# A hand-ordered fp32 transformer stack on one core: waits placed behind ready work, the decay product on row halves, and a new order at the start

## The chip, the cores and the metric

The kernel runs on one core of one Trainium2 chip, in fp32 throughout. The metric is the time of one execution on the device in microseconds (us). TensorE is called PE here, its weight loads PEld, VectorE DVE, ScalarE ACT, GpSimd POOL, SyncE SP. Each engine runs its own instruction list in order; semaphores tie the lists together.

## The reference, cut to what matters

256 tokens of width 1024 go through three layers. The first has an attention with a bias by distance, a pooling branch and a convolutional feed-forward part; the second ("even") has a forgetting attention ("fox", 8 heads) and a sliding-window attention with sinks ("swa", 8 heads), then a feed-forward part; the third ("odd") has an attention over the keys that an index score selects, then a mixture of 8 experts. Each layer's norm is modulated by vectors computed from a conditioning row `c` (the "ada" weights).

```python
def even_layer(x, c, cos, sin, ada_w, ada_b, ...):
    sh_m, sc_m, g_m, sh_f, sc_f, g_f = ada_modulation(c, ada_w, ada_b)
    h = rms_norm_2(x, norm_mix) * (1 + sc_m) + sh_m
    fq, fk, fv, fgl, sq, sk, sv = _split(h @ w_in, EVEN_SPLITS)
    log_f = jax.nn.log_sigmoid((fgl + forget_b).astype(jnp.float32))
    o_fox = forgetting_attention(heads(fq), heads(fk), heads(fv), log_f)   # scores + cumulated log_f
    o_swa = sliding_window_sink_attention(apply_rope(heads(sq), cos, sin), apply_rope(heads(sk), cos, sin), heads(sv), sinks)
    x = x + g_m * (jnp.concatenate([o_fox, o_swa], axis=-1) @ w_out)
    h = rms_norm_2(x, norm_ffn) * (1 + sc_f) + sh_f
    return x + g_f * swiglu(h, ffn_gate, ffn_up, ffn_down)
# odd_layer: q, k, v, iq, ik, iw = split(h @ w_in); o = dsa_attention(...);
#            x + g_f * moe_swiglu(h, ...), the sum over 8 experts of gate * swiglu
```

## The kernel before

Activations stand transposed: 8 chunks of 128 features by 256 tokens (`x`, `h`). Weights come through a ring of 24 slots of 512 KB, which SP fills in a fixed order and PE frees. A "unit" is a projection onto 128 features: 8 matmul blocks of 128x256, one per chunk of `h`. An fp32 matmul is two passes, and the trace counts each pass as one matmul. Results go to PSUM banks; ACT mostly copies them out (`take`, L1367) and so frees the bank.

The order of the work is written by hand, one program for each engine; units and the banks they use are numbered in `plan_units`. The places that matter here, with the lines of the profile:

- **Start.** SP first loads the conditioning row, the table of columns `cols` and the positions, then `x`, the identity, and the ring. DVE computes the angles of the rotation in a chain of ten operations that each wait for the one before (L1985 to L1993), then the sums of squares (L1712), then for each chunk c two modulation columns (L1728; each waits for one ring slot) and the product of `x` with the norm (L1717). ACT takes sine and cosine (L1524 to L1528), loads the table of Sqrt (L1373), takes the norm's root (L1400), and then scales and shifts each chunk into `h` (L1416). PE sums the squares (L767), multiplies the bias table (L1014), spreads the norm over the partitions (L777), and begins the q and k projections (L1024) as the chunks of `h` come. The chunks are not used evenly: with the first four chunks come 4, 12, 8 and 8 passes, and after chunk 3, 16 passes that need no later chunk.
- **Attention** (`attend`). Per pair of heads: scores (L865), for fox a second product that adds the decay (L872, 72 partitions deep, of which rows 0 to 7 and 64 to 71 carry data), softmax on DVE and ACT, transposes of the probabilities (L881), values (L894, L898). Other units (`between`) and the first steps of the output projection (`early_out`, L826) are put between. In the last turns there are no more scores to compute, and both transposes of neighbouring heads stand with nothing between them.
- **Raw units** (`raw_units`): after a feed-forward part the first two units of the next layer are multiplied with the unnormed input (L786) while the norm's sum (L767) and spread (L777) are made. The 8-wide products "fgl" and "iw" (L732, with a transpose, L747) come right after.
- **Odd attention.** Eight units "dq" are rotated: ACT makes four shifted copies of the bank (L1633), then takes the bank (L1367), and DVE rotates (L1825 to L1829); DVE also picks the keys (L2131, L2134).
- **Experts** (`expert_pass`): 8 passes; at the end of pass 0 DVE copies the turned selection (L2367) and then turns the hidden rows (L2244), which the next pass's first product on PE (L1283) waits for.

## Time and profile before

| quantity | value |
|---|---|
| median of 3 runs | 1267.29 us (1265.4 to 1267.48) |
| the profiled execution | 1263.85 us |
| its span in the trace | 1262.2 us |
| PE busy | 1229.3 us (97%) |
| DVE, ACT, POOL busy | 671.6 us (53%), 277.8 us (22%), 88.5 us (7%) |
| bytes moved by DMA | 368.78 MB, mean 292 GB/s |

The profiled execution is one execution; it took 3.4 us less than the median of the three runs. Its span is 1.65 us shorter than its time. In rows of the timeline the columns are start, duration, engine, line, operation, output<-inputs, size, count of merged instructions, and in brackets the idle time just before and what ended it. The ends of matmuls are modelled: eight passes given as 0.93 us are followed by the next row 0.86 us after their start.

### The profile page before, as it was taken

The page shows a single profiled execution, that of the slowest core. Times are in us where ns is not written, and L with a number is a line of the kernel's source. Part 1 is how long each engine was busy: PE and PEld are TensorE (multiplying, and loading weights), DVE is VectorE, ACT ScalarE, POOL GpSimd, SP SyncE. Part 2 cuts the span into 40 slices and gives each one's busy share as a digit, 9 for nine tenths or more (in the row PEclk, how much of TensorE's full clock was granted, in tenths as well). Part 3 has the DMA queues.
Part 4 walks back from the last instruction along what each step waited for, and adds up shares of the span by engine and source line. Part 5 has one row for each costly group of instructions (what it writes and reads, how often), then busy time and mean ns, then how long its engine had stood idle before and what let it go on. Part 6 is the DMA issues. An engine that isn't in the chain of part 4 may idle for free.

```text
span 1262.2 us, 26659 instructions
## 1 busy us (share of the span) xinstructions
PE 1229.3 (97%) x10620; PEld 936.9 (74%) x10620; DVE 671.6 (53%) x1672; ACT 277.8 (22%) x739; POOL 88.5 (7%) x157
## 2 busy tenths in 40 slices
PE   6999999999999999999999999999999999999997
PEld 4758888999999767789999997776654455455445
DVE  5455563888888735546776777883541011101104
ACT  4332203212111414540000004275300000000001
POOL 0100000000000000000000000100021100110120
PEclk9999999999999999999999999999999999999999
DMA  9999884577777583146777785795599999999993
GB/s 355 414 399 412 334 283 149 176 273 269 267 276 277 199 314 103 34 167 217 260 277 278 269 316 186 296 375 128 222 383 396 420 399 397 400 422 399 397 399 151
DMA packets 74822, 368.78 MB, mean 292 GB/s; under 512 B 8740, under 2 KB 8996, under 8 KB 49979
## 3 DMA queue, kind: packets, MB, share of 16 engines
q1 hardware_dynamic: 56594, 271.22, 57.3%
q0 software_dynamic: 18160, 96.64, 20.2%
q8 instruction: 45, 0.74, 0.2%
q14 instruction: 23, 0.18, 0.0%
HBM read 347.76 MB, written 20.06 MB: 291 GB/s over the span
## 4 chain that ended last, share of the span: by engine, by line
PE 92%; DVE 3%; DMA 2%; ACT 1%; SPq 1%; issue 1%; DVEq 0%
PE banks L957 21%; PE banks L697 16%; PE banks L1283 13%; PE banks L944 12%; PE banks L1332 9%; PE banks L1307 5%; PE banks L722 4%; PE banks L826 2%; PE banks L786 2%; PE banks L1024 2%; PE banks L881 1%; DMA side<-ada 1%; PE banks L865 1%; DMA ring<-stream 1%; PE banks L894 1%; DVE side L1728 1%
## 5 line engine op out<-in xcount | busy, mean ns | idle before, releaser
L1728 DVE CUSTOM_DVE_ANT_0 side<-side 128x1024 f32<-128x1024 f32 x128 | 151.1, 1220 | 32.6 <-DMA side<-ada 32.5
L1283 PE MATMUL banks<-ring,arena 128*32 128x512 f32 x1536 | 166.3, 592 | 1.6 <-DVE arena L2244 1.6
L944 PE MATMUL banks<-arena,ring 128*128 128x256 f32 x704 | 158.6, 379 | 0.0
L944 PEld LDWEIGHTS banks<-arena,ring 128*128 128x128 f32 x704 | 130.7, 190 | 16.1
L697 PE MATMUL banks<-h,ring 128*128 128x256 f32 x640 | 141.8, 380 | 0.3
L1283 PEld LDWEIGHTS banks<-ring,arena 128*32 128x32 f32 x1536 | 51.5, 110 | 111.4 <-issue 110.2
L697 PEld LDWEIGHTS banks<-h,ring 128*128 128x128 f32 x640 | 120.4, 190 | 18.4 <-issue 2.2
L2347 DVE TENSOR_TENSOR arena<-arena,banks 128x256 f32<-128x256 f32 (+1 forms) x48 | 15.2, 330 | 179.0 <-ACT arena L1665 178.9
L697 PE MATMUL banks<-arena,ring 128*128 128x256 f32 x384 | 84.3, 380 | 0.7 <-ACT arena L1464 0.5
L957 PEld LDWEIGHTS banks<-h,ring 128*128 128x128 f32 x672 | 81.4, 192 | 2.2
L614 POOL DMA_DIRECT2D side<-ada x64 | 34.0, 532 | 687.7 <-DVE msum L1728 678.2
L957 PE MATMUL banks<-arena 128*128 128x128 f32 x672 | 81.9, 275 | 0.0
L957 PE MATMUL banks<-arena,ring 128*128 128x128 f32 x672 | 81.9, 275 | 0.0
L957 PE MATMUL banks<-h,ring 128*128 128x128 f32 x672 | 81.8, 275 | 0.0
L697 PEld LDWEIGHTS banks<-arena,ring 128*128 128x128 f32 x384 | 72.5, 190 | 11.8 <-DVE x L1838 1.0
L1665 ACT ACTIVATE arena<-banks 128x256 f32<-128x256 f32 (+1 forms) x48 | 13.5, 318 | 303.4 <-PE banks L1283 253.1
L957 PEld LDWEIGHTS banks<-arena 128*128 128x128 f32 x672 | 78.4, 192 | 0.0
L957 PEld LDWEIGHTS banks<-arena,ring 128*128 128x128 f32 x672 | 78.4, 192 | 0.0
L1503 ACT ACTIVATE arena<-banks 128x128 f32<-128x128 f32 x42 | 11.7, 278 | 263.6 <-PE banks L957 263.6
L1307 PE MATMUL banks<-ring,arena 128*32 128x192 f32 x1536 | 63.9, 326 | 0.0
L1332 PE MATMUL banks<-side,arena 128*32 128x256 f32 x1152 | 63.7, 379 | 0.0
L1307 PEld LDWEIGHTS banks<-ring,arena 128*32 128x32 f32 x1536 | 51.6, 110 | 15.1 <-issue 4.7
(332 smaller groups left out, 1553.3 us busy)
## 6 DMA issues: line engine op xcount, KB each, us to landing
ring<-stream SPq DMA_DIRECT2D x247, 512.0 KB, 5.5
ring<-experts SPq DMA_DIRECT2D x96, 1024.0 KB, 18.9
side<-ada POOLq DMA_DIRECT2D x64, 1024.0 KB, 7.6
side<-experts SPq DMA_DIRECT2D x24, 1024.0 KB, 20.5
arena<-experts SPq DMA_DIRECT2D x8, 1024.0 KB, 21.9
yrows<-side POOLq DMA_DIRECT2D x1, 6144.0 KB, 42.7
hrows<-side POOLq DMA_DIRECT2D x1, 5632.0 KB, 23.4
arena<-lasts SPq DMA_DIRECT2D x8, 512.0 KB, 22.2
```

The costliest lines, as they stand in the source:

```text
L614: pool.dma_start(ada_slot[:, v % 2, :], ada[bass.ds(v + 8 * i, 1)].rearrange("a p r n -> p (a r n)")).then_inc(ada_full[v % 2], 16)
L697: last = pe.matmul(bank(u, a, a + T), ring[:, s, (k0 + kc) * P:(k0 + kc + 1) * P], moving[:, kc, :], start=(kc == 0), stop=(kc == kn - 1))
L722: last = pe.matmul(bank(u, at, at + width), h[:, kc, tile * P:(tile + 1) * P], ring[:, s, (kc % per) * width:(kc % per + 1) * width], star ...
L786: ins = pe.matmul(banks[:, b, 0:RAW], ring[:, pos % RING, k * P:(k + 1) * P], raw[:, k, :], start=(k == 0), stop=(k == KC - 1))
L826: last = pe.matmul(bank(u, (c % 2) * T, (c % 2 + 1) * T), ring[:, u.pos % RING, k * P:(k + 1) * P], moving[:, k, :], start=(k == 0 and c % ...
L944: last = pe.matmul(banks[:, 4 + c // 2, (c % 2) * T:(c % 2 + 1) * T], ring[:, s, c * P:(c + 1) * P], hid[:, j % 2, :], start=first and c % ...
L957: last = pe.matmul(banks[:, b, at * P:(at + 1) * P], weights[:, k * P:(k + 1) * P], moving[:, k, :], start=(start and k == 0), stop=(stop ...
L1024: ins = pe.matmul(bank(u, (n % 2) * T, (n % 2 + 1) * T), ring[:, u.pos % RING, k * P:(k + 1) * P], h[:, k, :], start=(k == 0 and n % 2 == ...
L1283: ins = pe.matmul(banks[BLOCK * j:BLOCK * (j + 1), t, :], hg[:, t, k, :], ring[:, m, (j % 2) * 512:(j % 2 + 1) * 512], start=(k == 0), sto ...
L1307: ins = pe.matmul(banks[BLOCK * j:BLOCK * (j + 1), BLOCKS + t, 0:2 * NARROW], hg[:, t, k, :], flat[:, at:at + 2 * NARROW], start=(k == 0), ...
L1332: ins = pe.matmul(banks[BLOCK * q:BLOCK * (q + 1), 6 + t // 2, (t % 2) * T:(t % 2 + 1) * T], mhidT[:, t, BLOCK * c:BLOCK * (c + 1)], moe_s ...
L1728: dve.tensor_tensor_reduce(weights, weights, cond[:, 0 if layer0 else 1, :], 1.0, 0.0, ALU.mult, ALU.add, accum_out=msum[:, n:n + 1]).then ...
```

## The change

Eight edits, all in the order or the shape of instructions, none in what is computed:

1. Start: SP loads `x` and the identity ahead of `cols` and the positions. The angle chain on DVE goes from the head of its list to behind the columns and norm of chunk 2. PE spreads the norm ahead of the bias table product. ACT does the root and all of `scale_shift(0)` before sine and cosine.
2. First attention: transposes of a pair's first head stand ahead of the gate units while scores of a later pair remain; ACT's order follows.
3. Raw units: two more blocks of the second unit stand ahead of the wait for the norm's squares; one whole unit goes ahead of "fgl" ("iw"), and another ahead of its transpose.
4. Fox decay: 40 rows for each head instead of 72, a pair's two heads in different halves of the partitions (rows 0 to 39 and 64 to 103), and one matmul of each head in turn. The data are laid out as for L865, whose two heads also stand in different halves.
5. The wait for the taken values `fv` goes from ahead of the even attention to the first fox pair's values.
6. Last turns of the even and odd attention: a step of `early_out` stands between the two transposes; the last step is split in two halves of its columns around the values.
7. `take_query`: ACT first takes the bank, and makes the four shifted copies from the copy in SBUF.
8. First expert pass: DVE turns the hidden rows before it copies the selection.

```diff
@@ start: SP, PE, ACT, DVE
             sp.dma_start(condrow, cond_d[0:1, :]).then_inc(cond_in, 16)
-            sp.dma_start(cols[:, :], cols_d).then_inc(cols_in, 16)
-            sp.dma_start(posi, pos_d).then_inc(cols_in, 16)
             sp.dma_start(x[:, 0:4, :], xT[:, 0:4, :]).then_inc(x_in, 16)
...
             sp.dma_start(mats[:, 0:P], mats_d[:, 0:P]).then_inc(ident_in, 16)
+            sp.dma_start(cols[:, :], cols_d).then_inc(cols_in, 16)
+            sp.dma_start(posi, pos_d).then_inc(cols_in, 16)
...
+            pe.wait_ge(ident_in, 16)
+            norm_spread(0)
             pe.wait_ge(s_bias, 16)
             pe.matmul(banks[:, 7, :], table[:, 512:], table[:, 0:512], start=True, stop=True).then_inc(s_early, 1)
-            pe.wait_ge(ident_in, 16)
-            norm_spread(0)
...
-            act.wait_ge(s_rope_dve, 9)
+            act.wait_ge(consts_set, 2)
+            load_table(ACT.Sqrt)
+            root(0)
+            act.wait_ge(s_rope_dve, 1)
+            scale_shift(0)
+            act.wait_ge(s_rope_dve, 10)
             act.activation(sin[:, :], ang, ACT.Sin).then_inc(s_rope_act, 1)
...
                 norm_chunks(0, c, c + 1)
+                if c == 2:
+                    angles()
@@ raw units
+                for k in range(2):
+                    raw_block(b.bank, b.pos, r, k)
                 begin(U["stat", r])
                 norm_sum(r)
...
             raw_units(2, ("fq", 0), ("fq", 1))
+            one(("fq", 2), r=2)
             few_outputs("fgl", 2)
-            one(("fq", 2))
+            one(("fq", 3))
             few_per_token("fgl")
-            one(("fq", 3))
             feature_units("fk", 4)
@@ fox decay
                     for a in pair:
-                        for lo, hi, n in ((0, HALF, HALF), (HALF, TRI, T)):
-                            ins = pe.matmul(banks[:, score_bank(a.n), lo:hi], cum[:, n - HALF:n], sel[:, a.i, 0:n],
-                                            start=False, stop=bool(lo))
+                        rows = slice(64 * a.half, 64 * a.half + 40)
+                        ins = pe.matmul(banks[:, score_bank(a.n), 0:HALF], cum[rows, 0:HALF], sel[rows, a.chunk, 0:HALF],
+                                        start=False, stop=False)
+                    for a in pair:
+                        rows = slice(64 * a.half, 64 * a.half + 40)
+                        ins = pe.matmul(banks[:, score_bank(a.n), HALF:TRI], cum[rows, HALF:T], sel[rows, a.chunk, 0:T],
+                                        start=False, stop=True)
                         ins.then_inc(s_score, 1)
@@ attend: transposes and steps
-                    first = heads is first_heads
-                    if 1 <= m <= len(pairs) and not first:
+                    steps = between.get(2 * m, []) + between.get(2 * m + 1, [])
+                    ahead = m + 1 >= len(pairs)
+                    if 1 <= m <= len(pairs) and not ahead:
                         transposes(pairs[m - 1][0])
-                    for step in between.get(2 * m, []) + between.get(2 * m + 1, []):
+                    for step in steps[:1] if m > len(pairs) else steps:
                         step()
-                    if 1 <= m <= len(pairs) and first:
+                    if 1 <= m <= len(pairs) and ahead:
                         transposes(pairs[m - 1][0])
                     if m >= 2:
                         values(pairs[m - 2])
+                    for step in steps[1:] if m > len(pairs) else []:
+                        step()
@@ take_query on ACT
-                act.wait_ge(*u.done)
+                take(u, dqT[:, c, :], 0, T)
+                act.wait_ge(*taken(u))
...
-                    act.activation(ropet[to, c % 3, :], banks[at, u.bank, 0:T], ACT.Copy, scale=1.0 if j % 2 else -1.0).then_inc(s_shift, 1)
-                take(u, dqT[:, c, :], 0, T)
+                    act.activation(ropet[to, c % 3, :], dqT[at, c, :], ACT.Copy, scale=1.0 if j % 2 else -1.0).then_inc(s_shift, 1)
@@ first expert pass on DVE
+                rows_turned(p)
                 if first:
                     dve.wait_ge(s_picktr, 2)
                     dve.tensor_copy(pickT[:, :, P:T], banks[:, 4, 0:BLOCKS * P].rearrange("p (a n) -> p a n", n=P)).then_inc(s_pickT_dve, 1)
-                rows_turned(p)
```

DVE's list, the start of the kernel before: the angle chain (`arena`, `half_pi`, `negsink`) stands first, then `ghalf`, the sums of squares and the first modulation column.

```order
L1985 CAST arena<-arena 128x256
L1986 TENSOR_SCALAR arena<-arena,vectors 128x256
L1987 TENSOR_SCALAR arena<-arena 128x256
L1988 TENSOR_SCALAR arena<-arena 128x256
L1990 SCALAR_TENSOR_TENSOR arena<-arena 128x256 x3
L1991 TENSOR_SCALAR arena<-arena 128x256
L1992 MEMSET half_pi 128x1
L1993 TENSOR_SCALAR negsink<-vectors 128x8
L1995 SCALAR_TENSOR_TENSOR ghalf<-vectors 128x8
L1712 TENSOR_TENSOR h<-h 128x256 x6
L1728 ISA ring,msum<-ring,side 128x1024
```

DVE's list of the changed kernel around the same chain, from the norm product of chunk 2 (L1733 there) to the first column of chunk 3 (L1744 there).

```order
L1733 TENSOR_TENSOR h<-x,banks 128x256
L2001 CAST arena<-arena 128x256
L2002 TENSOR_SCALAR arena<-arena,vectors 128x256
L2003 TENSOR_SCALAR arena<-arena 128x256
L2004 TENSOR_SCALAR arena<-arena 128x256
L2006 SCALAR_TENSOR_TENSOR arena<-arena 128x256 x3
L2007 TENSOR_SCALAR arena<-arena 128x256
L2008 MEMSET half_pi 128x1
L2009 TENSOR_SCALAR negsink<-vectors 128x8
L1744 ISA ring,msum<-ring,side 128x1024
L1744 ISA msum 128x1
```

The whole chain now stands between chunk 2's norm product and chunk 3's two columns.

ACT's list of the kernel before, where the copies of q and k end (L1541, L1542), the first half of v is taken (L1367) and the root of the q and k norms follows (L1549).

```order
L1541 ACTIVATE arena<-banks 128x256
L1542 ACTIVATE arena<-banks 128x256
L1367 ACTIVATE arena<-banks 128x512
L1549 ACTIVATE var<-banks,eps 128x512 x2
L1367 ACTIVATE arena<-banks 128x512
```

The same place on ACT in the changed kernel (L1557, L1558, L1382 and L1565 there).

```order
L1557 ACTIVATE arena<-banks 128x256
L1558 ACTIVATE arena<-banks 128x256
L1382 ACTIVATE arena<-banks 128x512
L1565 ACT_TABLE_LOAD
L1565 ACTIVATE var<-banks,eps 128x512 x2
L1382 ACTIVATE arena<-banks 128x512
```

Since sine and cosine now come after the Sqrt of the norm, the compiled list holds a second load of the Sqrt table at this place (and one of the sine's table ahead of the sine).

PE's list of the kernel before, from the norm's squares in the even layer's raw units (L767) to the units fq 3 and fk 0 to 3 (the last row merges them).

```order
L786 MATMUL banks<-logit,ring 128x257 x6
L767 MATMUL banks<-ones,h 128x1 x4
L786 MATMUL banks<-logit,ring 128x257 x4
L777 MATMUL banks<-constants,var 128x128 x2
L786 MATMUL banks<-logit,ring 128x257 x6
L732 MATMUL banks<-h,vectors 32x256 x8
L697 MATMUL banks<-h,ring 128x256 x8
L747 MATMUL banks<-constants,logit 128x8 x2
L697 MATMUL banks<-h,ring 128x256 x40
```

The same place on PE in the changed kernel (every line here is one higher: L787, L768, L778, L733, L698, L748).

```order
L787 MATMUL banks<-logit,ring 128x257 x8
L768 MATMUL banks<-ones,h 128x1 x4
L787 MATMUL banks<-logit,ring 128x257 x4
L778 MATMUL banks<-constants,var 128x128 x2
L787 MATMUL banks<-logit,ring 128x257 x4
L698 MATMUL banks<-h,ring 128x256 x8
L733 MATMUL banks<-h,vectors 32x256 x8
L698 MATMUL banks<-h,ring 128x256 x8
L748 MATMUL banks<-constants,logit 128x8 x2
L698 MATMUL banks<-h,ring 128x256 x32
```

One full unit (8 blocks) moved ahead of the 8-wide product and one ahead of its transpose, and two raw blocks moved ahead of the norm's sum.

## Rows read from the trace of the kernel before

**Rows 1.** The page, part 4: the chain that ended last, by engine.

```profile
PE 92%; DVE 3%; DMA 2%; ACT 1%; SPq 1%; issue 1%; DVEq 0%
```

**Rows 2.** Timeline, DVE, the start: angle chain and modulation columns.

```profile
4.80 0.29 DVE L1985 CAST arena<-arena 128x256 f32<-128x256 int32 x1 [4.80 <-DMA arena<-positions]
...
8.00 0.17 DVE L1993 TENSOR_SCALAR negsink<-vectors 128x8 f32<-128x8 f32 x1
...
24.43 1.22 DVE L1728 CUSTOM_DVE_ANT_0 ring<-ring,side 128x1024 f32<-128x1024 f32 x1
...
26.72 0.42 DVE L1717 TENSOR_TENSOR h<-x,banks 128x256 f32<-128x256 f32 x1
...
29.35 1.23 DVE L1728 CUSTOM_DVE_ANT_0 ring<-ring,side 128x1024 f32<-128x1024 f32 x1 [2.21 <-DMA ring<-stream]
```

**Rows 3.** Timeline, PE, the q and k projections.

```profile
18.86 5.85 PE L1024 MATMUL banks<-h,ring 128*128 128x256 f32 x16 [1.30 <-ACT h L1416]
25.29 1.99 PE L1024 MATMUL banks<-h,ring 128*128 128x256 f32 x8 [0.58 <-ACT h L1416]
27.91 22.71 PE L1024 MATMUL banks<-h,ring 128*128 128x256 f32 x104 [0.63 <-ACT h L1416]
```

**Rows 4.** Windows at the end: busy time by engine, then PEclk, DMA share, GB/s.

```profile
1254.90:1258.80 3.90, 0.00 (x0) 0.00 (x0) 3.59 (x8) 3.07 (x12) 0.00 (x0) 1.00 0.16 61
1258.90:1262.20 3.30, 0.00 (x0) 0.00 (x0) 0.78 (x2) 0.00 (x0) 0.00 (x0) 0.50 0.63 234
```

**Rows 5.** Timeline: the q and k norms' first root, and a table load later.

```profile
58.40 0.69 ACT L1549 ACTIVATE var<-banks,eps 128x512 f32<-128x512 f32 x1 [0.27 <-PE banks L1045]
59.13 0.30 PEld L722 LDWEIGHTS banks<-ring,h 128*128 128x128 f32 x2 [0.23 <-ACT var L1549]
...
82.56 1.28 ACT L1564 ACT_TABLE_LOAD   x1
83.86 1.06 ACT L1564 ACTIVATE side<-side 128x1024 f32<-128x1024 f32 x1
```

**Rows 6.** Timeline, ACT and PE, after the first raw units; and the page, part 5.

```profile
433.00 4.04 ACT L1416 ACTIVATE h<-h,mod,avec 128x256 f32<-128x256 f32 x8 [2.54 <-DVE h L1717]
...
434.99 2.73 PE L732 MATMUL banks<-h,vectors 128*32 128x256 f32 x16
...
L1332 PE MATMUL banks<-side,arena 128*32 128x256 f32 x1152 | 63.7, 379 | 0.0
```

**Rows 7.** Timeline, PE, the first fox pair: scores and decay.

```profile
474.76 0.93 PE L865 MATMUL banks<-arena 64*128 64x128 f32 x8 [0.92 <-ACT arena L1367]
475.62 1.58 PE L872 MATMUL banks<-arena 72*128 72x128 f32 x8
```

**Rows 8.** Timeline, PE, the even attention's last turns.

```profile
525.43 0.52 PE L881 MATMUL banks<-constants,logit 128*128 128x128 f32 x3 [0.67 <-ACT logit L1443]
...
536.49 1.78 PE L826 MATMUL banks<-arena,ring 128*128 128x256 f32 x7 [0.51 <-ACT arena L1464]
```

**Rows 9.** Timeline, PE, the first attention.

```profile
118.92 0.52 PE L881 MATMUL banks<-constants,logit 128*128 128x128 f32 x3 [0.67 <-DVE logit L1781]
```

**Rows 10.** Timeline, DVE and PE, from the first rotated query to the first transposes.

```profile
818.37 0.43 DVE L1825 TENSOR_TENSOR arena<-arena,sin 128x256 f32<-128x256 f32 x1 [2.63 <-ACT arena L1633]
...
833.12 0.55 PE L881 MATMUL banks<-constants,logit 128*128 128x128 f32 x3
```

**Rows 11.** Timeline, ACT and PE, where the odd layer's output projection begins.

```profile
850.14 1.57 ACT L1633 ACTIVATE arena<-banks 32x256 f32<-32x256 f32 x4
...
852.22 1.10 PE L826 MATMUL banks<-arena,ring 128*128 128x256 f32 x4 [1.30 <-issue]
```

**Rows 12.** Timeline, expert pass 0 to 1; and the page, part 5.

```profile
950.39 0.56 DVE L2367 COPY arena<-banks 128x384 f32<-128x384 f32 x1 [14.34 <-PE banks L1317]
...
951.97 2.35 PE L1283 MATMUL banks<-ring,arena 128*32 128x512 f32 x20 [1.62 <-DVE arena L2244]
...
L1283 PE MATMUL banks<-ring,arena 128*32 128x512 f32 x1536 | 166.3, 592 | 1.6 <-DVE arena L2244 1.6
```

More of the change, by code:

```diff
@@ L818, in step @@
                     pe.wait_ge(s_o, pairs_done + k + 1)
-                    for c in range(4):
+                    for c in columns:
                         out_block(name, moving, c, k)
@@ L889, in values @@
                     pe.wait_ge(*taken(U["sv"]))
+                if pair[0].kind == "fox" and pair[0].i == 0:
+                    pe.wait_ge(*taken(U["fv", 0]))
+                    pe.wait_ge(*taken(U["fv", 1]))
                 if done >= 1:
@@ L1136, in _ @@
                        8: [sv_unit]}
-            for k in range(7):
+            for k in range(6):
                 m = max(5, 3 + k)
                 between[2 * m] = between.get(2 * m, []) + [early_out("eo", oT2, 4, k)]
+            between[18] = [early_out("eo", oT2, 4, 6, columns) for columns in ((0, 1), (2, 3))]
             attend(even_heads, between)
@@ L1194, in _ @@
             between = {2 * (c - 4): [dq(c)] for c in range(4, 8)}
-            for k in range(7):
+            for k in range(6):
                 m = max(4, 3 + k)
                 between[2 * m] = between.get(2 * m, []) + [early_out("oo", dqT, 12, k)]
+            between[18] = [early_out("oo", dqT, 12, 6, columns) for columns in ((0, 1), (2, 3))]
             attend(odd_heads, between)
@@ L1450, in attend @@
                         exps(pairs[m][0])
-                        if first:
-                            exps(pairs[m][1])
-                    if first:
+                    if first and m + 1 >= len(pairs):
                         for step in steps:
@@ L1457, in attend @@
                         transposed(pairs[m - 1][0])
-                    if m < len(pairs) and not first:
+                    if m < len(pairs):
                         exps(pairs[m][1])
+                    if first and m + 1 < len(pairs):
+                        for step in steps:
+                            step()
                     if m >= 2:
@@ L1608, in _ @@
             norm(4)
+            take(U["iq", 1], iqT[:, 1, :], 0, T)
             take(U["iw"], few, 0, T)
-            take(U["iq", 1], iqT[:, 1, :], 0, T)
+            take(U["iq", 2], iqT[:, 2, :], 0, T)
             take(U["iwT"], iws.rearrange("p a n -> p (a n)"), 0, 16, scale=float(8 ** -0.5 * 64 ** -0.5))
-            for c in range(2, 4):
-                take(U["iq", c], iqT[:, c, :], 0, T)
+            take(U["iq", 3], iqT[:, 3, :], 0, T)
             for c in range(2):
@@ L2449, in _constants @@
     pool = np.ascontiguousarray(pool.reshape(2, P, 4, T).transpose(1, 0, 2, 3))
-    sel = np.zeros((72, 8, T), np.float32)
-    sel[np.arange(8), np.arange(8)] = 1.0
-    sel[64 + np.arange(8), np.arange(8)] = 1.0
+    sel = np.zeros((FORGET, 4, T), np.float32)
+    for half in range(2):
+        for at in (64 * half, 64 * half + 32):
+            sel[at + half + 2 * np.arange(4), np.arange(4)] = 1.0
     inv_freq = (np.float32(10000.0) ** (-np.arange(32, dtype=np.float32) / np.float32(32))).astype(np.float32)
```

86 lines of the change are left out of this document (44 added, 42 removed).

## Prediction

> **What bounds the kernel now.** I read the chain that ended last first: TensorE's own work is 92% of it, and DMA, DVE and ACT together about 6% [rows 1]. So only two things can move the time: PE's own passes, and the places where PE stands idle for another engine. I then went along PE's timeline and took each idle stretch with what ended it. The stalls are many and small, 0.5 to 1.6 us each, and lie where the change works: before the first fox pair, between neighbouring transposes, at the start of the odd output projection, between expert passes 0 and 1 [rows 7 to 9, 11, 12]. The modelled ends of matmuls run a little late (0.93 us given for 0.86 us [rows 7]), so each idle shown is about 0.1 us too small. A full-rate 256-column pass is 22.71/104 = 0.218 us [rows 3]; a block is 0.44, a unit of 8 blocks 3.5 us.
>
> **The start: a loss, +3.4 us.** Before, the angle chain runs from 4.80 to 8.17, 3.4 us, while DVE has nothing else to do but wait for the load of x [rows 2]. After, it stands between the norm product of chunk 2 and the columns of chunk 3. Does a wait hide it there? In the rows of before DVE starts the column of chunk 3 at 24.43, with no idle ahead of it, and ends the norm product of that chunk at 27.14; ACT's scaling follows and PE starts on chunk 3 at 27.91 [rows 2, 3]. The ring had delivered already. The next wait for a slot, 2.21 us, comes only behind it, at 29.35 [rows 2]. So chunk 3 comes 3.4 us later, at 31.3. Chunk 4 is late by 3.4 less that wait, 1.2 us, and PE has 24 passes (5.2 us) of other work from chunk 3 to there, so only PE's start on chunk 3 counts. From there PE ran 104 passes without an idle [rows 3]: it cannot catch up, and all 3.4 us go into the end. The two first chunks come up to 2.7 us earlier (x first, no sine ahead of the norm's root), but chunk 2 waits for its ring slots in any case, so PE only idles elsewhere. Bounds: 0 (chain hidden) to +3.6 (ten linked operations with their gaps). I take 3.4.
>
> **A table load on the path, +1.0 us.** The compiled order of the changed kernel loads the Sqrt table between the take of v's first half and the root of the q and k norms. Before, ACT stands idle 0.27 us there, starts the root at 58.40, and PE's next weight load waits for it (0.23 us) [rows 5]. A load took 1.28 us [rows 5], less the idle of 0.27: +1.0. The other new load, ahead of the sine, comes when all chunks are scaled; what follows it on ACT is the copy of the bias rows, some 2.6 us late (the load and three activations of 256 columns), whose results are needed tens of us later. If that cover fails, it costs at most those 2.6 us.
> The Trainium skill ("ScalarE: Activation LUTs", section "What ACT_TABLE_LOAD costs") puts a drain of 1380 ns behind the load of 1283 ns, which speaks against the change: the term would be +2.4. The trace agrees on the load, but shows the next operation 0.02 us after the load's end [rows 5], so I leave the drain out.
>
> **First attention, -0.7.** A transpose of a second head waited 0.67 us for DVE with nothing between [rows 9]; the four gate units now stand between the two. Bounds 0 (a softmax late at the earlier place of the first head) and -0.8.
>
> **After the raw units, -2.6 in the even layer.** Eight chunks of h come from ACT between 433.00 and 437.04 [rows 6]. The 16 passes of the 8-wide product start at 434.99 and take 2.73 us [rows 6], though such a product, on 32 columns of the array, goes at 63.7/1152 = 0.055 us a pass when nothing holds it [rows 6], or 0.9 us: it is paced by ACT. Before, product and unit end at 434.99 + 2.73 + 3.5 = 441.2. After, the unit goes first, and its last block follows the last chunk: 437.04 + 0.44 = 437.5; then the product, 438.4. That is 2.8 us. The wait for the norm's squares, which the two raw blocks fill, lies inside this: the chunks come no earlier. Off goes up to 0.4 us where the next unit finds its bank just being copied. Taken -2.6, bounds -2.0 and -3.1.
>
> **The same place in the odd layer, -1.1.** The gain on PE is the same, but behind it DVE works through the key selection from 818.37 without a long break until the first transposes at 833.12 [rows 10]. That chain starts when ACT's shifted copies of the first query are there, and ACT now takes the bank first, 0.4 us more. Nothing kept is one bound, 2.6 - 0.4 = 2.2 the other; I see no row nearer to either, and take the middle.
>
> **Fox decay, -2.6.** The decay product took 1.58 us for a pair, and the scores of the same columns, with the two heads in different halves of the rows, 0.93 [rows 7]. Four pairs: 4 x 0.65 = 2.6. The trace shows no 40-row matmul; the bounds are nothing (two halves do not run side by side) and -2.6, and the nearest row is the score of the very same pair. DVE gets two small operations more for the sums and two for the table, of the size of work that it does in its idle half.
>
> **The wait for fv, -0.9.** The first pair waited 0.92 us for ACT's take [rows 7]. The values that need it come a whole pair later.
>
> **The ends of the attentions, -1.2 each.** In the even one: two stalls of 0.67 us between neighbouring transposes (at 525.43 and, alike, at 529.62) and 0.51 us ahead of the last output step [rows 8], 1.85 in all. A step of 4 blocks (1.8 us) now fills each. What is late next: the step itself waits for ACT's copy of the values just ahead, which was covered by a pair of transposes before; I put 0.3 us on each of two places. 1.85 - 0.6 = 1.2; bounds -0.4 and -1.9. The odd one shows the same pattern with the same idles. Together -2.4.
>
> **Start of the odd output projection, -1.3.** PE stands 1.30 us ahead of the first step [rows 11]. Its bank is that of the last query, and ACT's four shifted copies (1.57 us, to 851.7) come ahead of the take; with the take first, the bank is free about 1.5 us earlier. Bounds -0.8 and -1.5.
>
> **First expert pass, -1.6.** DVE stood 14.34 us idle, then copied the selection (0.56), then turned the rows, and PE waited 1.62 us for the turn [rows 12]. The turn needs only the gathered rows, and can lie in those 14 us; PE then needs only the selection's copy, and that later. If the rows land late, nothing is won. The weights are no obstacle: of 1536 matmuls that read them from the ring, all idle ahead is this 1.6 us [rows 12].
>
> **Sum.** +3.4 + 1.0 - 0.7 - 2.6 - 1.1 - 2.6 - 0.9 - 2.4 - 1.3 - 1.6 = -8.8. With about 0.1 us of hidden idle in each of nine stalls, -9.7. The profiled execution would go from 1263.85 to 1254.2; the median of the runs stands 3.4 us above the profiled execution, so 1267.29 - 9.7 = 1257.6. All bounds taken at their poor end (start +3.6, load and its cover +3.6, gains of 2.0, 0.8, 0.8 and 0.8 alone, after the raw units, at fv, at the two ends and at the output projection) give about +3; all at the good end about -16.
>
> **Rivals.**
> *The clock falls in the new gap.* PE idles from 27.3 (end of chunk 2 [rows 3]) to 31.3, 4.0 us. At the end of the kernel PE does nothing from 1254.9; the granted clock shows 1.00 to 1258.8 and 0.50 from 1258.9 [rows 4]: it fell to the lower of its two levels (1.2 of 2.4 GHz) 4.0 us after PE's last work. So the new gap is just at the edge. Price: the first 16 passes of the projections took 5.85 us [rows 3] where 3.5 is the full rate, 2.4 us for one climb. Time 1260.0. The Trainium skill ("TensorE: Matmul & The Clock Gate", section "HAM oscillation — how this bites in real kernels") warns against idle gaps of this order between bursts of matmuls, since the clock then falls; by that rule 1260.0 would be the forecast. The tail agrees that it falls, but shows a gap of the same length that did not yet do it.
> *The change does not cost at the start.* If chunk 3's slots come later than before (the ring's loads are issued behind two more small ones, or x first draws the bandwidth), the chain lies in that wait. Then 1254.2. Against it: chunk 3's columns found their slots there, and the same bytes are loaded ahead of them as before.
> *Stalls move instead of going.* The filled waits come back at the next step: each step or unit put in front ends in a bank that ACT must still copy, and the softmax of the next head is no earlier. If half of the 14.2 us of gains go so, the net is 4.4 - 7.1 = -2.7: 1264.6. For it speaks DVE's chain in the odd layer [rows 10].
> *Slower.* The clock falls in the gap and stays low. Each pass at the lower level costs 0.218 us more; all 104 passes up to the end of q and k would cost 22.7 us, 1280. It turns slower than before once 45 passes (9.7 us) run low, and by more than 0.2% from 56. Against it: the climb at 18.86 was over within 16 passes.
>
> **How the numbers follow.** The sum as it stands 0.50; clock falls once 0.20; no cost at the start 0.09; stalls move 0.15; slower 0.06. What a measurement of this kernel can tell from no change is 0.2%, 2.5 us. Faster: the first three cases and half of the fourth, 0.87; within 0.2%: the other half, 0.08; slower 0.05. The range 1251 to 1264 takes the first three cases with their bounds and the better part of the fourth.
>
> **What the profile after would show.** Right: PE's row of 104 passes starting near 31.3 with an idle of 4 us; an ACT_TABLE_LOAD just ahead of the q and k root, and PE's idle there near 1.2; the decay rows at about 0.9 a pair; no idle ahead of the first fox pair, the odd layer's first output step and pass 1 of the experts; PE's busy time less by 2.6 to 4. Wrong: passes of 0.43 us behind 31.3 (the clock); the columns of chunk 3 preceded by a wait for the ring (no cost); new idles ahead of L829's steps or of the unit behind each filled place (moved stalls). The forecast fails most easily at the fox term, if two 40-row halves don't run side by side, and at the four places where I trust ACT's copies to be early enough.

## The result and the profile after

The changed kernel takes 1256.93 us in the median of 4 runs (1255.1 to 1258.46), the kernel before 1266.89 beside it: a ratio of 0.9923, 95% interval [0.9905, 0.994], faster by 0.6 to 1.0%. A second set gave 1257.04 against 1266.53, ratio 0.992 [0.9904, 0.9936]; there one of twelve runs of the kernel before took 2159.77 us at a granted clock of 0.558 and is left out of its median. The forecast was 1257.6. The profiled execution took 1257.12, its span is 1255.5 us.

The page of the changed kernel, part 4, the chain by engine:

```profile
PE 90%; DVE 5%; DMA 3%; ACT 1%; issue 1%; SPq 1%; DVEq 0%; POOLq 0%; ACTq 0%
```

DVE has more of the chain than before [rows 1], and the timeline shows where. DVE and PE at the start, the counterpart of [rows 2, 3]:

```profile
20.28 1.23 DVE L1744 CUSTOM_DVE_ANT_0 ring<-ring,side 128x1024 f32<-128x1024 f32 x1 [2.27 <-DMA ring<-stream]
...
23.04 0.29 DVE L2001 CAST arena<-arena 128x256 f32<-128x256 int32 x1
...
26.44 1.22 DVE L1744 CUSTOM_DVE_ANT_0 ring<-ring,side 128x1024 f32<-128x1024 f32 x1
...
29.07 1.22 DVE L1744 CUSTOM_DVE_ANT_0 ring<-ring,side 128x1024 f32<-128x1024 f32 x1
```

```profile
23.90 1.99 PE L1037 MATMUL banks<-h,ring 128*128 128x256 f32 x8 [1.23 <-ACT h L1431]
29.93 25.16 PE L1037 MATMUL banks<-h,ring 128*128 128x256 f32 x104 [4.04 <-ACT h L1431]
```

The chain sits between 23.04 and 26.44, 3.4 us, and behind it the first column of chunk 3 starts with no wait; so does that of chunk 4, at 29.07. PE has an idle of 4.04 us ahead of chunk 3. The same 104 passes then take 25.16 us, not 22.71. The windows of that stretch (the last columns are PEclk, DMA share, GB/s) say why:

```profile
27.00:30.00 3.00, 0.07 (x1) 0.08 (x1) 3.00 (x6) 1.28 (x3) 0.00 (x0) 0.68 1.02 407
...
32.00:34.00 2.00, 2.00 (x6) 1.55 (x6) 0.58 (x1) 0.49 (x1) 0.00 (x0) 0.50 1.01 404
34.00:38.00 4.00, 4.00 (x18) 3.46 (x17) 3.95 (x8) 1.57 (x4) 0.00 (x0) 0.89 1.03 410
```

The granted clock fell to its lower level inside the idle and came back only after 34 us: PE did some 5 us of its passes at half rate.

The root of the q and k norms, answering [rows 5]; the load follows the take, and PE waits for the root 0.87 us:

```profile
62.61 1.28 ACT L1565 ACT_TABLE_LOAD   x1
...
63.90 0.69 ACT L1565 ACTIVATE var<-banks,eps 128x512 f32<-128x512 f32 x1
64.64 0.30 PEld L723 LDWEIGHTS banks<-ring,h 128*128 128x128 f32 x2 [1.27 <-ACT var L1565]
64.64 1.55 PE L723 MATMUL banks<-ring,h 128*128 128x512 f32 x3 [0.87 <-ACT var L1565]
```

The first attention, DVE and PE: the wait of [rows 9] is at another transpose, behind DVE columns that waited for an ada load.

```profile
122.52 1.23 DVE L1744 CUSTOM_DVE_ANT_0 side<-side 128x1024 f32<-128x1024 f32 x1 [4.86 <-DMA side<-ada]
...
125.62 0.55 PE L888 MATMUL banks<-constants,logit 128*128 128x128 f32 x3 [0.72 <-DVE logit L1797]
```

After the raw units of the even layer, ACT and PE, answering [rows 6]: the unit goes at full rate, the 8-wide product behind it takes 1.07 us, not 2.73, and no row of PE here waits.

```profile
438.35 4.04 ACT L1431 ACTIVATE h<-h,mod,avec 128x256 f32<-128x256 f32 x8 [2.54 <-DVE h L1733]
...
434.49 1.02 PE L768 MATMUL banks<-ones,h 128*128 128x1 f32 x8
...
439.38 3.77 PE L698 MATMUL banks<-h,ring 128*128 128x256 f32 x16
443.08 1.07 PE L733 MATMUL banks<-h,vectors 128*32 128x256 f32 x16
```

The first fox pair, answering [rows 7]: scores with no wait ahead, then the decay in two merged rows, and the next pair's scores 0.65 us after the decay's start, where it was 1.5.

```profile
476.76 0.93 PE L868 MATMUL banks<-arena 64*128 64x128 f32 x8
477.52 0.39 PE L875 MATMUL banks<-arena 40*128 40x128 f32 x4
477.74 0.60 PE L879 MATMUL banks<-arena 40*128 40x256 f32 x4
478.17 0.82 PE L868 MATMUL banks<-arena 64*128 64x128 f32 x8
```

The end of the even attention [rows 8]: the waits between transposes are gone, one is now ahead of an output step. In the odd layer the first transposes wait for DVE, and the first output step [rows 11] no longer waits.

```profile
527.90 1.99 PE L829 MATMUL banks<-arena,ring 128*128 128x256 f32 x8 [0.63 <-ACT arena L1480]
...
829.52 0.55 PE L888 MATMUL banks<-constants,logit 128*128 128x128 f32 x3 [0.50 <-DVE logit L1797]
...
847.15 3.19 PE L829 MATMUL banks<-arena,ring 128*128 128x256 f32 x14
```

Expert pass 0 and the step to pass 1 [rows 12], PE and DVE:

```profile
939.81 0.59 PE L1347 MATMUL banks<-side,arena 128*32 128x256 f32 x2 [0.73 <-issue]
...
945.31 3.21 PE L1298 MATMUL banks<-ring,arena 128*32 128x512 f32 x28
```

```profile
942.28 0.98 DVE L2269 STREAM_TRANSPOSE arena<-logit 128x768 f32<-128x768 f32 x1 [12.68 <-DMA logit<-hrows]
945.42 0.56 DVE L2393 COPY arena<-banks 128x384 f32<-128x384 f32 x1 [2.16 <-PE banks L1332]
```

DVE has the rows turned by 943.26, and PE starts pass 1 at 945.31. The gathered rows land only just before 942.3, so this edit had a margin of 2 us and not of 14.

**Where the time went.** The same instruction's start in both profiles, before and after, and what changed from one point to the next:

| place | before | after | difference | step |
|---|---|---|---|---|
| v's first pass (end of q and k) | 50.47 | 54.92 | +4.45 | +4.45 start |
| PE behind the q and k root | 59.15 | 64.64 | +5.49 | +1.04 table load |
| first unit after the first attention | 157.71 | 163.06 | +5.35 | -0.14 first attention |
| unit behind the transpose of fgl | 445.40 | 448.27 | +2.87 | -2.5 raw units, even |
| first fox scores | 474.76 | 476.76 | +2.00 | -0.9 wait for fv |
| transposes behind the fourth fox pair | 495.14 | 493.98 | -1.16 | -3.2 fox decay |
| last output step, even | 536.49 | 534.36 | -2.13 | -1.0 end of even attention |
| first transposes, odd | 833.12 | 829.52 | -3.60 | -1.5 raw units, odd |
| first output step, odd | 852.22 | 847.15 | -5.07 | -1.5 query taken first |
| last output step, odd | 877.60 | 871.27 | -6.33 | -1.3 end of odd attention |
| pass 1 of the experts | 951.97 | 945.31 | -6.66 | -0.3 (144 passes of pass 0 on weights in `side` held, +1.5; rows turned first -1.7; the rest of pass 0 -0.1) |

The held passes are those around the idle of 0.73 us: from their first row to the transposes behind them they take 9.36 us (930.98 to 940.34), and took 7.88 before (937.42 to 945.30).

The two profiled executions stand 6.7 us apart, the medians 10.0. The missing 3.3 us are looked for below.

### The profile page after: what moved, and what is told of

Its sections match the earlier page's. It is cut to its first block, busy times and chain, and to the rows that moved or that the text cites. A ratio compares the mean times of both kernels' runs of the same rounds, so it can differ in the third digit from the quotient of the medians.

```text
span 1255.5 us, 26666 instructions
## 1 busy us (share of the span) xinstructions
PE 1226.2 (98%) x10620; PEld 931.8 (74%) x10620; DVE 671.1 (53%) x1676; ACT 281.2 (22%) x741; POOL 88.4 (7%) x157
## 4 chain that ended last, share of the span: by engine, by line
PE 90%; DVE 5%; DMA 3%; ACT 1%; issue 1%; SPq 1%; DVEq 0%; POOLq 0%; ACTq 0%
PE banks L970 21%; PE banks L1298 13%; PE banks L698 13%; PE banks L957 12%; PE banks L1347 9%; PE banks L1322 5%; PE banks L723 4%; PE banks L829 2%; PE banks L787 2%; PE banks L1037 2%; DMA side<-ada 2%; PE banks L888 1%; DVE side L1744 1%; DMA ring<-stream 1%; PE banks L868 1%; PE banks L904 1%
## 5 line engine op out<-in xcount | busy, mean ns | idle before, releaser
L1744 DVE CUSTOM_DVE_ANT_0 side<-side 128x1024 f32<-128x1024 f32 x128 | 151.0, 1219 | 31.4 <-DMA side<-ada 31.0
L698 PE MATMUL banks<-h,ring 128*128 128x256 f32 x640 | 142.3, 381 | 0.3
L698 PEld LDWEIGHTS banks<-h,ring 128*128 128x128 f32 x640 | 119.7, 190 | 18.9 <-issue 1.8
L1298 PEld LDWEIGHTS banks<-ring,arena 128*32 128x32 f32 x1536 | 49.7, 110 | 111.5 <-issue 110.4
L698 PE MATMUL banks<-arena,ring 128*128 128x256 f32 x384 | 84.3, 380 | 0.7 <-ACT arena L1480 0.5
L698 PEld LDWEIGHTS banks<-arena,ring 128*128 128x128 f32 x384 | 72.5, 190 | 11.8 <-DVE x L1853 1.0
L1322 PEld LDWEIGHTS banks<-ring,arena 128*32 128x32 f32 x1536 | 50.4, 110 | 16.3 <-issue 4.8
```

The costliest lines, as they stand in the source:

```text
L698: last = pe.matmul(bank(u, a, a + T), ring[:, s, (k0 + kc) * P:(k0 + kc + 1) * P], moving[:, kc, :], start=(kc == 0), stop=(kc == kn - 1))
L1298: ins = pe.matmul(banks[BLOCK * j:BLOCK * (j + 1), t, :], hg[:, t, k, :], ring[:, m, (j % 2) * 512:(j % 2 + 1) * 512], start=(k == 0), sto ...
L1322: ins = pe.matmul(banks[BLOCK * j:BLOCK * (j + 1), BLOCKS + t, 0:2 * NARROW], hg[:, t, k, :], flat[:, at:at + 2 * NARROW], start=(k == 0), ...
L1744: dve.tensor_tensor_reduce(weights, weights, cond[:, 0 if layer0 else 1, :], 1.0, 0.0, ALU.mult, ALU.add, accum_out=msum[:, n:n + 1]).then ...
```

## The experiments

All but one were timed beside the kernel before on the same chip; beside the first four its median was 1265.93 us, beside the next four 1266.53, beside the last three, on another chip, 1265.96. Each diff is against the changed kernel unless it says otherwise.

**The chain behind chunk 3.**

```diff
-                if c == 2:
+                if c == 3:
                     angles()
```

> The angle chain stands behind chunk 3 instead of chunk 2, nothing else. My theory: the start loses twice, by chunk 3 coming late behind the chain and by the clock that falls in the gap which this makes on PE. Chunk 3's norm product would then end near 25.8 us, PE start on it near 26.5 with an idle below 1 us, and the granted clock stay at 1.00 there; chunk 4 comes near 32.6, where PE would wait some 0.9 us. The 104 passes would end near 50 us (55.0 in the changed kernel): 5.0 us less, 1251.9 us. Rival, the clock falls at the start whatever the gap: only the 3.4 us of the chain come back, and the passes behind chunk 3 still take 0.43 us: 1253.5. Rival, the chain only moves its cost to chunk 4: no change, 1256.9.

1251.08 us, ratio 0.9876 [0.9857, 0.9896]. PE on chunk 3 and chunk 4:

```profile
26.45 5.45 PE L1037 MATMUL banks<-h,ring 128*128 128x256 f32 x24 [0.63 <-ACT h L1431]
32.48 17.53 PE L1037 MATMUL banks<-h,ring 128*128 128x256 f32 x80 [0.58 <-ACT h L1431]
49.85 7.03 PE L723 MATMUL banks<-ring,h 128*128 128x512 f32 x16
```

PE starts at 26.45, the passes end 5.07 us earlier (49.85 for 54.92), and all go at 0.22 us. Both rivals fall.

**The same, and the Sqrt table loaded early.**

```diff
             act.wait_ge(s_rope_act, 3)
+            act.activation(warm[:, 7:8], eps[:, :], ACT.Sqrt)
```

> The same, and ACT uses Sqrt once on one column right after the cosine, so that its table is loaded while ACT waits for the q projections. My theory: no table load stands ahead of the root of the q and k norms any more, PE's idle of 0.87 us there goes, and 1.05 us come off beyond the run without it: about 1250.9 us. Rival: the load is not what PE waits for there, and the time is that of the run without it.

1249.35 us, ratio 0.9859 [0.984, 0.9878]; 1.7 us below the run without it, where the runs of each lie within 2.3 us. The trace is sharper than the times: ACT's root comes right behind PE's products again, and PE's wait of 0.87 us is gone.

```profile
57.62 0.69 ACT L1566 ACTIVATE var<-banks,eps 128x512 f32<-128x512 f32 x1 [0.27 <-PE banks L1058]
58.36 0.30 PEld L723 LDWEIGHTS banks<-ring,h 128*128 128x128 f32 x2 [0.23 <-ACT var L1566]
```

**PE kept busy in the gap.**

```diff
                 for n in range(there):
                     qk_block(n, k)
+                if k == 2:
+                    for _ in range(9):
+                        pe.matmul(banks[:, 5, 0:T], ident, h[:, 0, :], start=True, stop=True)
```

> The changed kernel, with nine matmuls of 128x256 more on PE behind chunk 2's blocks (18 passes, 3.9 us at the full rate, into a bank that a later matmul starts afresh; nothing reads them). They fill PE's idle before chunk 3 and do not make chunk 3 earlier. My theory: the clock fell because PE stood idle there, so it now stays at 1.00; PE starts on chunk 3 at 29.9 as before, and the 104 passes take 22.7 us instead of 25.2: 2.4 us less, 1254.5. Rival, the granted clock falls there for another reason: the row stays at 25.2 us or more, and the time at 1256.9 or above.

1255.09 us, ratio 0.9902 [0.9885, 0.9919].

```profile
25.64 4.05 PE L1051 MATMUL banks<-h,constants 128*128 128x256 f32 x18
29.84 22.71 PE L1037 MATMUL banks<-h,ring 128*128 128x256 f32 x104 [0.15 <-ACT h L1434]
```

Chunk 3 comes at the same time as in the changed kernel, but the 104 passes take 22.71 us. So the idle brought the clock down, and the fall costs 2.45 us between these two traces (1.8 us between the medians); the rest of the loss is the chunk's lateness.

**The start undone.** (The four places of the start as before; the other seven edits stand.)

```diff
-                if c == 2:
-                    angles()
+            link(dve.tensor_copy(posf, posi), s_rope_dve)
...
             for n in range(1, SUMMED):
                 square_sum(0, n)
```

> The changed kernel with its start undone: loads, order on PE, DVE and ACT at the start as in the kernel before; all other edits stand. My theory: the start costs 4.45 us up to the end of the q and k projections and 1.05 us at the table load, so this kernel is 5.5 us faster than the changed one, 1251.4, and about 15.5 us faster than the kernel before by the medians (12.2 by the two profiles). Rival, x first pays at a place I have not seen: less than 2 us from the changed kernel, 1255 to 1257.

1251.49 us, ratio 0.9876 [0.9857, 0.9895]: 5.4 to 5.6 us below the changed kernel.

**The start alone.** (The kernel before with the four places of the start from the changed kernel; the diff is against the kernel before.)

```diff
-            link(dve.tensor_copy(posf, posi), s_rope_dve)
...
                 norm_chunks(0, c, c + 1)
+                if c == 2:
+                    angles()
```

> The kernel before with the changed start alone (loads, order on PE, DVE and ACT). My theory: 2.0 us from the chain, 2.4 from the clock, 1.05 from the table load, all kept to the end: 5.5 us slower than the kernel before, 1271.4 by a median of 1265.9. Rival, a wait of the first attention for the ada loads takes it up: less than 2 us slower.

1271.88 us, ratio 1.0039 [1.0024, 1.0053]: slower, by 5.4 us in the medians (3.0 to 6.7 by the interval). Its 104 passes took 25.19 us behind an idle of 4.04. Taken with the run above, the first edit loses some 5 us of its own and the other seven win 14.

**The changed kernel again**, with no edit.

> The changed kernel once more, beside the other runs of this call, as their measure. The two profiled executions stand 6.7 us apart, the medians 10.0. If the profile of the kernel before was a fast one of its kind, this run's time is again near 1256.9 us and its ratio near 0.992; its profile again has the idle of 4 us before chunk 3 and the granted clock at 0.5 for some 7 us behind it. The idle of 0.73 us among the expert matmuls, which nothing in the records ends, comes again at the same place if it is of the change, and not if it is of one execution.

1257.04 us. Its profile has the idle of 4.04 us and 25.44 us for the 104 passes, and no idle among the expert matmuls: that one was of one execution. The 144 passes around it are uneven in all kernels: 7.88 us in four of the thirteen profiles (the kernel before, the changed kernel with the chain behind chunk 3, with PE kept busy, and with the first attention as before), 8.2 to 9.1 in eight, 9.36 in the first profile of the changed kernel.

**The decay on 72 rows, heads in turn.**

```diff
-FORGET = 104
+FORGET = 72
...
-                        rows = slice(64 * a.half, 64 * a.half + 40)
+                        rows = slice(0, FORGET)
-                        ins = pe.matmul(banks[:, score_bank(a.n), 0:HALF], cum[rows, 0:HALF], sel[rows, a.chunk, 0:HALF],
+                        ins = pe.matmul(banks[:, score_bank(a.n), 0:HALF], cum[rows, 0:HALF], sel[rows, a.i, 0:HALF],
...
```

> The changed kernel, with the decay product on 72 rows as before, in the changed order of the heads. My theory: what saves is that the two heads stand in different halves of the rows and run side by side; then the decay of a pair goes from 0.65 us back to 1.5, four times, and the kernel is 3.4 us slower: 1260.3. Rival, it is the order of the heads (one matmul of each in turn): no change, 1256.9.

1259.74 us, ratio 0.9948 [0.9928, 0.9968], against 0.992 for the changed kernel in the same set. The trace, first pair:

```profile
475.47 0.93 PE L868 MATMUL banks<-arena 64*128 64x128 f32 x8
476.33 0.71 PE L875 MATMUL banks<-arena 72*128 72x128 f32 x4
476.87 1.03 PE L879 MATMUL banks<-arena 72*128 72x256 f32 x4
477.83 0.93 PE L868 MATMUL banks<-arena 64*128 64x128 f32 x8
```

From the decay's start to the next scores 1.50 us, 0.65 in the changed kernel: the order of the heads gives nothing. Even the scores ahead hold PE 0.10 us longer when the decay behind them is not on halves (0.86 for 0.76). Fewer rows without the two halves were not run. The rows speak against a gain from depth alone: passes of 256 columns come 0.24 us apart here at 72 rows (four in 0.96 us), and 0.218 apart at 128 rows [rows 3]. At that rate a pair's four passes of 256 columns and four of 128 would take 1.3 us one after another, by estimate; they take 0.65 in the changed kernel, so the two heads do run side by side.

**The chain behind the last chunk.**

```diff
-                if c == 2:
-                    angles()
+            angles()
             dve.wait_ge(s_xn, 8)
...
             act.activation(t5rows, banks[:, 7, :], ACT.Copy, scale=1 / SCALE).then_inc(s_early, 1)
+            act.wait_ge(s_rope_dve, 10)
+            act.activation(sin[:, :], ang, ACT.Sin).then_inc(s_rope_act, 1)
...
+            act.activation(warm[:, 7:8], eps[:, :], ACT.Sqrt)
```

> The changed kernel with the angle chain behind the last chunk's norm product, where DVE waits for the q and k norms, sine and cosine behind the copy of the bias rows, and the Sqrt table loaded right after. My theory: nothing at the start waits for the chain; PE waits for no chunk behind chunk 3, the clock stays at 1.00, no table load stands ahead of the q and k root. Behind chunk 3 at 26.4 us the 104 passes run without an idle to 49.0: 0.75 us less than with the chain behind chunk 3 and the early load (1249.35 measured), 1248.6. Rival, the sine at that place holds up the copies of q and k on ACT, and PE waits for them: more than 1250.

1248.81 us, ratio 0.9863 [0.9842, 0.9883]: 8 us below the changed kernel. By the ratio it is level with the chain behind chunk 3 and the early load (0.9859); in the traces the projections of v start 0.95 us earlier than there (48.74 for 49.69).

```profile
26.19 22.71 PE L1037 MATMUL banks<-h,ring 128*128 128x256 f32 x104 [0.63 <-ACT h L1431]
```

**The kernel before again**, with no edit, for its profile.

> The kernel before once more, for its profile. Its runs lie between 1264.4 and 1270.2 us, with a mean granted clock of 0.999 in the fastest and 0.993 to 0.996 in the slowest, and the profile that the prediction rests on is the fastest of all (1263.85, 0.999). My theory: in most executions the clock falls for a few us at one or two of the waits that the change fills (the norm's sum in the raw units, near 429 or 772 us) or in the routing near 890 us, 1.7 us each, and the earlier profile had none of these; this profile then shows the granted clock below 1.00 in one such stretch, or, if it has none again, a time near 1264. Rival: the spread has nothing to do with these places, and a time above 1265.5 comes with a full clock there.

One execution, 1266.04 us. Windows around the odd layer's raw units, and PE there:

```profile
770.00:776.00 6.00, 5.09 (x20) 4.05 (x21) 1.38 (x4) 1.89 (x6) 0.00 (x0) 0.74 0.53 190
```

```profile
771.57 1.02 PE L767 MATMUL banks<-ones,h 128*128 128x1 f32 x8 [0.91 <-DVE h L1712]
772.46 3.41 PE L786 MATMUL banks<-logit,ring 128*128 128x257 f32 x8
```

The granted clock fell behind the wait for the squares and the eight one-column passes, and the eight passes that took 1.98 us in the first profile took 3.41. In the first profile the clock was full there. Up to the unit before, the two executions agree within 0.5 us. The profile of the start alone, which leaves the same wait unfilled, shows the fall too:

```profile
778.31 3.17 PE L786 MATMUL banks<-logit,ring 128*128 128x257 f32 x8
```

**The two raw blocks put back** (in the version with the chain behind the last chunk).

```diff
-                for k in range(2):
-                    raw_block(b.bank, b.pos, r, k)
                 begin(U["stat", r])
...
-                for k in range(2, 4):
+                for k in range(2):
                     raw_block(b.bank, b.pos, r, k)
                 norm_spread(r)
-                for k in range(4, KC):
+                for k in range(2, KC):
```

> The version with the angle chain behind the last chunk (1248.81), with the two raw blocks put back behind the wait for the norm's squares. The prediction held that this wait lies inside the time of the chunks of h and that filling it gives nothing by itself. My theory: at a full clock no difference at the unit behind it; what the filled wait gives is that PE's idle of 0.9 us ahead of one-column matmuls no longer lets the clock fall: 0 to 3.4 us slower, 1250 in the median, with a lower mean clock in the slower runs. Rival, the filled wait gives its full 1.08 us at each of the two places: 1251.0 at the same clock.

1251.7 us, ratio 0.9883 [0.9867, 0.9899], 2.9 us above the version it is made from (2.5 by the ratios, whose intervals overlap). PE at the even layer's place (clock full there), up to the 8-wide product of L733, in this kernel and then in the version it is made from:

```profile
427.18 1.02 PE L768 MATMUL banks<-ones,h 128*128 128x1 f32 x8 [0.91 <-DVE h L1727]
...
432.94 3.62 PE L698 MATMUL banks<-h,ring 128*128 128x256 f32 x16
436.49 1.07 PE L733 MATMUL banks<-h,vectors 128*32 128x256 f32 x16
```

```profile
426.95 1.02 PE L768 MATMUL banks<-ones,h 128*128 128x1 f32 x8
...
431.84 3.77 PE L698 MATMUL banks<-h,ring 128*128 128x256 f32 x16
435.54 1.07 PE L733 MATMUL banks<-h,vectors 128*32 128x256 f32 x16
```

The product starts 0.95 us later. Of this, 0.23 us were there ahead of it (the one-column passes of L768 start at 427.18 and 426.95), so the filled wait gives 0.72 us. My theory falls here: it gives this at a full clock. And in the odd layer the clock fell as well:

```profile
764.00:768.00 4.00, 4.00 (x15) 3.40 (x16) 0.17 (x1) 0.26 (x1) 0.00 (x0) 0.59 0.34 114
```

**The first attention's order as before.**

```diff
-                    ahead = m + 1 >= len(pairs)
+                    ahead = m + 1 >= len(pairs) or heads is first_heads
...
```

> The changed kernel with the first attention's order as before (gate units ahead of both transposes, ACT likewise). The trace of the changed kernel shows an idle of 0.72 us ahead of a transpose at 125.6 us in place of the one of 0.67 at 118.9 before. My theory: this edit gives nothing, since DVE's softmax there waits for the ada loads either way: within 1 us of the changed kernel, 1256 to 1258, with one idle of about 0.7 us among the transposes. Rival: it gives its 0.7 to 0.8 us and the idle at 125.6 has another cause, so that this kernel has both and is 0.8 us slower.

1255.66 us, ratio 0.9919 [0.9907, 0.9932], against 0.992 and 0.9923 for the changed kernel: no difference. PE waits once more at the old place:

```profile
123.41 0.52 PE L888 MATMUL banks<-constants,logit 128*128 128x128 f32 x3 [0.67 <-DVE logit L1796]
```

## Why the prediction was right, and where not

The time was right, 1257.6 forecast and 1256.93 measured, and no part had the wrong sign. But the sum reached it by steps of which some were off, and that it came within 0.7 us is in part luck: the start cost 1.1 us more than its two terms (+5.5 for +4.4), and the medians gained from falls of the clock elsewhere that no term had (below, the measure).

**The start.** The chain does cost its 3.4 us on chunk 3, as worked out, but the whole front moved 1.4 us earlier: chunk 2's first column starts at 20.28, before at 21.67, both times right behind a wait for the ring. Of the start's edits only the order of the loads can bear on that wait, since the ring's first filling waits for no engine; no run changed this order alone. I had called it worthless. So the lateness is 2.0 us and not 3.4. The clock's fall, which I gave one chance in five, came in all five profiled executions of kernels with that gap (the 104 passes took 24.3 to 25.4 us) and in none of the eight others, where the gap was filled or absent. The case that I put first held the start to +3.4; it was +4.45, of which 2.45 are the clock. So here the rival was right in its mechanism and its price (2.4 us), and its time of 1260.0 was 3 us too high; the price, though, was read from the first 16 passes at 18.86 [rows 3], where the clock's column still reads 1.00 (16 to 20 us), so no row of the clock shows a climb there. The step that failed is the reading of the tail [rows 4]: "fell 4.0 us after PE's last work" was taken as the length that an idle needs. In the changed kernel PE's last pass ended near 25.9 and the window from 27 to 30 has a mean clock of 0.68, so the fall came near 28.1, after some 2.2 us. By the Trainium skill's rule ("TensorE: Matmul & The Clock Gate", section "HAM oscillation — how this bites in real kernels", no long idles between bursts) the fall was to be expected, and the runs side with it: five idles of 4.04 us, five falls.

**The table load.** +1.04 for +1.0. The next operation starts 0.01 us after the load, so the drain that the Trainium skill ("ScalarE: Activation LUTs", section "What ACT_TABLE_LOAD costs") adds did not show here either. Loading it early takes it off the path. The cover of the bias rows held: the first attention behind it lost nothing (-0.14 in the table).

**First attention.** -0.7 forecast, -0.1 in the table and no difference in the run without this edit: the wait moved by some passes. DVE's columns for the ada loads stand ahead of the softmax there and waited 4.86 us for their load, so PE waits for DVE at one transpose or at another. That is my rival of the moved stalls, at this one place.

**Raw units.** -2.6 and -1.1 forecast, -2.5 and -1.5 measured. One sentence of it was wrong: that filling the wait for the squares gives nothing by itself. I let the unit end with the last chunk, at 437.5; but PE came to it only at 434.99 [rows 6] and needs 3.5 us for it, to 438.5. With the wait filled, PE and the chunks pace the unit within 0.2 us of each other; with the wait back, PE is the later one, and the run shows 0.72 us.

**Fox.** -2.6 forecast, -3.2 measured; mechanism right, size low, and past the bound of -2.6: the decay of the four pairs went from 1.4 to 1.5 us each to 0.65 to 0.76, less than the 0.86 of the scores that I took as the nearest row, and there is one more gain, some 0.1 us a pair, at the seam with the scores.

**The other gains** came within 0.3 us: wait for fv -0.9 (-0.9), ends of the attentions -1.0 and -1.3 (-1.2 each), with one wait of 0.63 us at a new place as priced, the first odd output step -1.5 (-1.3), rows turned first -1.7 (-1.6): the wait of 1.62 us is gone. These were read from one pair of traces; no run took these edits out one by one.

**The measure.** By the profiles the gain was 6.7 us, by the medians 10. The prediction rested on the fastest execution of the kernel before that was seen at all (1263.85; the others lie between 1264.0 and 1270.2). Two things in the profiles bear on the missing 3.3 us. The 144 expert passes were held 1.5 us in the profile of the changed kernel and not at all in that of the kernel before. And the odd layer's wait for the squares, which the change fills, goes with a fall of the clock: it came there in three of the four profiled executions of kernels that leave the wait unfilled (the eight passes took 3.41, 3.17 and 3.20 us for 1.98), and in none of the nine that fill it. The profile that the prediction rests on is the one of the four without it. A fall costs 1.7 us: from the eight passes to the 8-wide product 6.64 us, without it 4.96. As an estimate, 1.5 us and three quarters of 1.7 are 2.8 of the 3.3; four executions are few for such a share. By and large the runs with a lower mean clock are the slower ones (0.999 at 1264.4, 0.993 and 0.994 at 1269.5 and 1269.6).

## What to carry to other kernels

Work put behind "the next wait" has to be put behind a wait that is there: list the idle of the engine that takes it in, instruction by instruction, and move it to the longest one (here DVE's 16 us behind the last chunk) and not to the first gap by name. Price a new idle on PE twice, once for the work that comes late and once for the clock; filling it with dummy matmuls tells the two apart in one run. And before trusting a profile as the base of a sum, look whether its time and its mean clock are the middle of the runs or their edge.

## What the runs showed of the hardware that was not expected

- Behind an idle of 0.9 us on PE and 1 us of one-column passes the granted clock fell in three of four executions in the odd layer (0.74 in a window of 6 us, 0.59 in one of 4), and in none of the same four in the even layer, where PE's rows are alike. It also fell near 890 us, among the short matmuls of the routing, in four of the thirteen profiles (32 passes took 5.4 to 7.0 us for 3.78).
- The fall does not come at a fixed distance from the last work: near 2.2 us in one profile of the changed kernel; in the run with the decay on 72 rows the clock was still 1.00 from 27 to 30 us and 0.59 from 30 to 34, so it fell when PE was already at work again. The cost was 1.7 us there, and 1.6 to 2.7 in the others.
- Loading x and the identity ahead of the column table and the positions went with a use of chunk 2's ring slot 1.4 us earlier, though the same bytes are loaded ahead of it (it came at 19.95 to 20.28 in the ten profiles with the new start, at 21.16 to 21.67 in the three with the old).
- The 144 expert passes of the first pass on weights in `side` took 7.88 us in four profiles and up to 9.36 in the others, with no releaser in the records.
